# First product of three feed-forwards in seven half-size products for eight, in a fused two-block fp32 kernel on one core

## What is computed

```
def swiglu(h, w_in, w_out):
    a, b = h @ w_in[:, :D_FF], h @ w_in[:, D_FF:]      # D_FF = 2816, h is 512 x 1024
    return (silu(a) * b) @ w_out
```

## Time and profile before

| what | value |
|---|---|
| median of three executions | 3304.2 us (3299.51 to 3306.26) |
| span of the profiled execution | 3302.2 us |
| TensorE busy | 3203.2 us, 97% |
| VectorE, ScalarE, GpSimd busy | 48%, 34%, 13% |
| "ffn 0" on the trace | about 425 to 787 us |
| "ffn 1" | about 1136 to 1498 us |
| ("ffn2", 1) | about 2901 to 3281 us |

### The profile page before, as it was taken

The page is one execution under the profiler, slowest core; times in us unless marked ns, Lnnn a source line. Parts: engine busy times, 40 slices in busy tenths (PEclk is TensorE's granted clock), DMA queues, the critical chain, the costliest instruction groups (busy, mean ns, idle before and its releaser), DMA issues.

```text
span 3302.2 us, 45048 instructions
## 1 busy us (share of the span) xinstructions
PE 3203.2 (97%) x19414; PEld 2595.4 (79%) x19414; DVE 1573.5 (48%) x2498; ACT 1129.4 (34%) x1827; POOL 417.1 (13%) x622
## 2 busy tenths in 40 slices
PE   7999999999999999999999999999999999989999
PEld 5787888887887888887875677888887876668886
DVE  4646454446434654444246545343344437454544
ACT  6565532124434522223245443111112336431222
POOL 1302110002200300000010015000001311030000
PEclk9999999999999999999999999999999999999999
DMA  3111123223227322232243340222202222013221
GB/s 135 53 52 53 52 83 121 77 77 118 77 102 281 103 90 77 96 108 62 77 156 129 103 128 1 77 77 77 77 2 79 50 84 57 35 43 132 98 77 39
DMA packets 190743, 281.81 MB, mean 85 GB/s; under 512 B 19144, under 2 KB 122184, under 8 KB 190416
## 3 DMA queue, kind: packets, MB, share of 16 engines
q1 hardware_dynamic: 188368, 272.19, 24.8%
q10 hardware_dynamic: 2176, 6.73, 0.6%
HBM read 273.66 MB, written 2.10 MB: 84 GB/s over the span
## 4 chain that ended last, share of the span: by engine, by line
PE 90%; DVE 3%; ACT 3%; POOL 2%; issue 1%; DMA 1%; ACTq 0%; POOLq 0%; DVEq 0%; SPq 0%
PE ps L895 11%; PE ps L896 11%; PE ps L897 11%; PE ps L548 6%; PE ps L549 6%; PE ps L550 6%; PE ps L926 5%; PE ps L927 5%; PE ps L928 5%; PE ps L442 3%; PE ps L633 2%; PE ps L634 2%; PE ps L635 2%; PE ps L1533 2%; PE ps L1501 1%; PE ps L1709 1%
## 5 line engine op out<-in xcount | busy, mean ns | idle before, releaser
L451 ACT ACTIVATE R<-ring 128x2048 fp32r<-128x2048 f32 (+4 forms) x285 | 401.9, 1417 | 971.3 <-PE ps L928 345.0
L895 PE MATMUL ps<-R,R 128*128 128x512 f32 (+1 forms) x1760 | 654.3, 372 | 13.6 <-DVE R L810 8.6
L896 PE MATMUL ps<-R,R 128*128 128x512 f32 (+1 forms) x1760 | 650.3, 369 | 0.0
L897 PE MATMUL ps<-R,R 128*128 128x512 f32 (+1 forms) x1760 | 650.1, 369 | 0.0
L548 PE MATMUL ps<-R,R 128*128 128x512 f32 (+1 forms) x1016 | 395.9, 390 | 13.7 <-ACT U L451 4.0
L895 PEld LDWEIGHTS ps<-R,R 128*128 128x128 f32 x1760 | 333.2, 189 | 77.6 <-issue 13.0
L549 PE MATMUL ps<-R,R 128*128 128x512 f32 (+1 forms) x1016 | 379.2, 373 | 0.0
L550 PE MATMUL ps<-R,ringlo 128*128 128x512 f32 (+1 forms) x1016 | 378.4, 372 | 0.0
L897 PEld LDWEIGHTS ps<-R,R 128*128 128x128 f32 x1760 | 333.3, 189 | 56.2
L896 PEld LDWEIGHTS ps<-R,R 128*128 128x128 f32 x1760 | 333.4, 189 | 54.8 <-issue 0.5
L926 PE MATMUL ps<-R,R 128*128 128x512 f32 (+1 forms) x880 | 325.9, 370 | 0.9 <-DVE X L4029 0.9
(11 more groups left out here) (330 smaller groups left out, 4585.2 us busy)
## 6 DMA issues: line engine op xcount, KB each, us to landing
ring<-in_w_mod SPq DMA_DIRECT2D x24, 2048.0 KB, 9.8
ring<-in_ffn_w_in SPq DMA_DIRECT2D x44, 1024.0 KB, 11.9
ring<-in_w_ffn_in SPq DMA_DIRECT2D x44, 1024.0 KB, 12.2
ring<-in_ffn_w_out SPq DMA_DIRECT2D x10, 2048.0 KB, 8.0
ring<-in_w_ffn_out SPq DMA_DIRECT2D x10, 2048.0 KB, 8.0
ring<-in_dil_w_in SPq DMA_DIRECT2D x9, 2048.0 KB, 7.8
ring<-in_gdn_w_in SPq DMA_DIRECT2D x8, 2048.0 KB, 8.7
ring<-in_w_in SPq DMA_DIRECT2D x6, 1536.0 KB, 8.8
```

What stands on the lines that cost most here:

```text
L451: return act.e.activation(o, i, fn, **kw)
L895: pe.e.matmul(ps, w[0], x[0], start=(k == 0), stop=False)
L896: pe.e.matmul(ps, w[0], x[1], start=False, stop=False)
L897: t = pe.e.matmul(ps, w[1], x[0], start=False, stop=(k == 7))
```

## The change

"ffn 0", "ffn 1" and ("ffn2", 1) get functions of their own (`pe_ffn_s` and the like); ("ffn2", 0), with the context stream, stays. `FROM` says from which chunk on a chunk is made in the new way: chunk 2 in "ffn 0", chunk 3 in the other two. Chunks before it ("plain") are made as before, but with their own buffers `NT` for the high parts and the low part written in place into the ring slot.

From there on a chunk has two **units** (j = 0, 1). A unit takes the 2 x 2 blocks of the weights (k half by gate or other half) and of the activations (k half by 256-token half) and makes the four result blocks with seven products of 4 k-tiles by three matmuls of 128 x 256 instead of eight (Winograd's form): 84 half-width matmuls for 48 full-width ones. The seven weight factors are b11, b21, b22 of the weights themselves and t1 to t4, differences formed by GpSimd; the activation factors s1 to s4 are formed once for each feed-forward, in chunk FROM - 1, by VectorE and GpSimd. Products 1, 6, 7 and 4 pile up in one bank "a", and ScalarE copies ("snap") its state out between them; products 2, 5 and 3 have the banks "b", "c", "d", which VectorE adds in. Behind the seven products stand four output tiles of the chunk before.

```
+        def pe_unit(tag, c, j, between):
...
+            product(1, "a", True, False)
+            product(2, "b", True, True)
+            pe.wait_ge(*at("snap", tag, c, j, 0))
+            product(6, "a", False, False)
+            product(5, "c", True, True)
+            pe.wait_ge(*at("snap", tag, c, j, 1))
+            product(7, "a", False, False)
+            product(3, "d", True, True)
+            pe.wait_ge(*at("snap", tag, c, j, 2))
+            product(4, "a", False, True)
+            for i in range(4):
+                between(i)
+            if j:
+                pe.mark("gate up", tag, c)
+                pe.mark("ring read", (tag, "in", c))
```

GpSimd forms the factors of the next unit, ScalarE makes their high parts, VectorE the low parts:

```
+        def pool_factors(tag, c, j):
...
+            pool.wait_ge(*at("filled", (tag, "in", c)))
+            unit_free(pool, tag, c, j, 5)
+            op("t1", t1, b12, b11)
+            unit_free(pool, tag, c, j, 6)
+            pool.wait_ge(*at("factor", tag, c, j, "t1"))
+            op("t3", b12, b22, b12)
+            op("t2", t2, b22, t1)
+            pool.wait_ge(*at("factor", tag, c, j, "t2"))
+            op("t4", t4, b21, t2)
```

GpSimd's queue in the plain chunks and in the units (`unit_free` waits for "gate up" of the chunk when the unit before was plain):

```
+        def pool_ffn_s(tag, mid={}):
+            f = FROM[tag]
+            for c in range(f):
...
+                if c == f - 1:
+                    eng_shares(pool, tag, "s1")
+                    eng_shares(pool, tag, "s2")
+                pool_ffn_gate(tag, [S], c, 0, 0)
+                if (c, 1) in mid:
+                    mid[c, 1]()
+                if c == f - 1:
+                    eng_shares(pool, tag, "s4")
+                    pool_factors(tag, f, 0)
+                pool_ffn_gate(tag, [S], c, 1, 0)
+            for c in range(f, 11):
+                for j in range(2):
+                    pool_unit(tag, c, j, mid)
```

```
+        def dve_ffn_s(tag, take_out, then=None, early=None, mid={}, last=None):
...
+                if c == 0:
+                    dve_plain(tag, 1, 0)
+                if c == f - 1:
+                    eng_shares(dve, tag, "s3")
+                if c < f:
+                    dve_ffn_gate(tag, [S], c, 0, 0)
+                if 0 < c < f - 1:
+                    dve_plain(tag, c + 1, 0)
+                if c == f - 1:
+                    dve_share(tag, "s3")
+                    dve_share(tag, "s1")
+                if c < f:
+                    dve_ffn_gate(tag, [S], c, 1, 0)
+                elif c < 11:
+                    for j in range(2):
+                        dve_unit(tag, c, j, take_out)
+                if c < f - 1:
+                    dve_plain(tag, c + 1, 1)
+                if c in (0, 10):
+                    dve_out_lo(tag, c)
+                if c == 11 and early:
+                    early()
+                if c == 11:
+                    outs(10, border)
+                elif 0 < c < f:
+                    outs(c - 1)
+                if c == f - 1:
+                    dve_share(tag, "s2")
+                    dve_share(tag, "s4")
+                    for x in OPS:
+                        dve_factor(tag, f, 0, x)
+                if 0 < c < f:
+                    dve_out_lo(tag, c)
```

```
+        def act_out_hi(tag, c):
+            act.wait_ge(*at("filled", (tag, "out", c if c > 1 else 0)))
+            if c == 10:
+                act.wait_ge(*at("gate up", tag, 10))
+            elif c:
+                act.wait_ge(*at("down", tag, c - 1))
+            activate(WOH[c == 10], out_half(ring, tag, c), ACT.Copy).then_inc(*act.done("wo hi", tag, c))
```

More of the change, by code:

```diff
@@ L910, in pe_ffn_in @@
             pe.mark("gate up", tag, c)
+        FROM = {"ffn 0": 2, "ffn 1": 3, ("ffn2", 1): 3}
+        HALF = [slice(0, 256), slice(256, 512)]
+        NT = [[view(ru(o + 1024 * p, 1024), (8, 128)) for p in range(2)] for o in (22528, 28672)]
+        OPS = ("b11", "b21", "t2", "t1", "t3", "b22", "t4")
+        T_HI = {x: view(ru(o, 512), (4, 128)) for x, o in zip(
+            OPS, (22528, 23040, 23552, 24064, 28672, 29184, 29696))}
+        T_AT = {"t1": (31744, 31744), "t2": (32256, 32256), "t4": (8192, 30208)}
@@ new lines, in pe_unit, with product @@
+        def pe_unit(tag, c, j, between):
+            banks = {}
+            def product(i, x, first, last):
+                w, h = PRODUCTS[i]
+                if x not in banks:
+                    banks[x] = bank("sum", tag, c, j, x)
+                    PS.keep("sum", tag, c, j, x)
+                pe.wait_ge(*at("factor lo", tag, c, j, w))
+                if h in S_R:
+                    pe.wait_ge(*at("share lo", tag, h))
+                ps = banks[x][:, 0:256]
+                hi, lo = T_HI[w], factor(w, tag, c, j, True)
+                go_on = not first
+                for k in range(4):
+                    pe.e.matmul(ps, hi[:, k, :], share(h, 0)[:, k, :], start=(first and k == 0), stop=False, skip_group_check=go_on)
+                    pe.e.matmul(ps, hi[:, k, :], share(h, 1)[:, k, :], start=False, stop=False, skip_group_check=go_on)
+                    t = pe.e.matmul(ps, lo[:, k, :], share(h, 0)[:, k, :], start=False, stop=(k == 3), skip_group_check=go_on)
+                t.then_inc(*pe.done("unit", tag, c, j, i))
+                if last:
+                    PS.release("sum", tag, c, j, x)
+            product(1, "a", True, False)
[11 more added lines that the diff above has]
+            if j:
+                pe.mark("gate up", tag, c)
+                pe.mark("ring read", (tag, "in", c))
@@ new lines, in pe_out_one @@
+        def pe_out_one(tag, c, m, last):
+            ps = bank("product", tag, "out", c, m, 0)
+            pe.wait_ge(*at("wo lo", tag, c))
+            pe.wait_ge(*at("g lo", tag, c, 0, 1))
+            hi, lo = WOH[c == 10], out_half(ring_lo, tag, c)
+            for k in range(2):
+                w = [z[:, k, m * 128:(m + 1) * 128] for z in (hi, lo)]
+                x = [z[:, k, :] for z in GR_[0][c % 2]]
+                pe.e.matmul(ps, w[0], x[0], start=(k == 0), stop=False)
+                pe.e.matmul(ps, w[0], x[1], start=False, stop=False)
+                t = pe.e.matmul(ps, w[1], x[0], start=False, stop=(k == 1))
+            t.then_inc(*pe.done("product", tag, "out", c, m, 0))
+            if last and c == 10:
+                last(m)
+            if m == 7:
+                pe.mark("down", tag, c)
+                if c == 10:
+                    pe.mark("ring read", (tag, "out", 10))
+                    pe.mark("end", tag, "pe")
@@ new lines, in pe_ffn_s @@
+        def pe_ffn_s(tag, mid={}, between={}, last=None):
+            behind = (PS.i + 4) % 8
+            for c in range(12):
+                if c in mid:
+                    mid[c]()
+                if c == 0:
+                    pe_ffn_in(tag, [S], 0, between, 0)
+                elif c < FROM[tag]:
+                    pe_in_plain(tag, c)
+                elif c < 11:
+                    for j in range(2):
+                        pe_unit(tag, c, j, lambda i: pe_out_one(tag, c - 1, 4 * j + i, last))
+                    continue
+                if c:
+                    for m in range(8):
+                        pe_out_one(tag, c - 1, m, last)
+            while PS.i % 8 != behind:
+                PS.i += 1
@@ new lines, in act_plain, with dve_plain @@
+        def act_plain(tag, c, j):
+            for p in range(2):
+                act.wait_ge(*at("filled", (tag, "in", c)))
+                if c > 1:
+                    act.wait_ge(*at("product", "ffn", tag, c - 1, j, 0, 1))
+                elif j:
+                    act.wait_ge(*at("gate up", tag, 0))
+                activate(NT[j][p], column(ring, tag, c, j, p), ACT.Copy).then_inc(*act.done("plain hi", tag, c, j, p))
+        def dve_plain(tag, c, j):
+            for p in range(2):
+                dve.wait_ge(*at("plain hi", tag, c, j, p))
+                dve.e.tensor_tensor(column(ring_lo, tag, c, j, p), column(ring, tag, c, j, p), NT[j][p], SUB).then_inc(
+                    *dve.done("plain lo", tag, c, j, p))
@@ new lines, in pool_factors, with op @@
+        def pool_factors(tag, c, j):
+            def op(x, o, a_, b_):
+                pool.e.tensor_tensor(o, a_, b_, SUB).then_inc(*pool.done("factor", tag, c, j, x))
+            b11, b12, b21, b22 = (quarter(ring, tag, c, j, kh, p) for kh in range(2) for p in range(2))
+            t1, t2, t4 = (factor(x, tag, c, j, False) for x in ("t1", "t2", "t4"))
+            pool.wait_ge(*at("filled", (tag, "in", c)))
[7 more added lines that the diff above has]
+            op("t4", t4, b21, t2)
@@ L949, in dve_ffn_gate @@
             n, name = ns[s], (tag, c, j, s)
-            g, before = TG.take(*name)
+            if tag in FROM:
+                g, before = TG.tiles[j], TG.take_at([j], *name)[0]
+            else:
+                g, before = TG.take(*name)
             if c == 0 and tag in XRAW:
```

306 lines of the change are left out of this document (287 added, 19 removed).

## The result

| kernel | median | beside it, the kernel before | ratio, 95% interval |
|---|---|---|---|
| changed | 3325.7 us (3322.3 to 3328.4) | 3302.6 us | 1.0068 [1.0054, 1.0082] |

The account below looks back on a forecast made before the run. TensorE, busy 97% of the span, was taken to bound the kernel. Terms -41.0 - 0.7 + 13.7 + 14 + 18 + 10.5 + 9 = +23.5 on 3302.2, with 2 us to the median 3328; range 3294 to 3344.

Parts of the forecast that it names:

- 0.82 us a unit: In each unit's first product, 84 half-width matmuls replace 48 full-width: 10.88 to 10.06 us; 50 units, -41.0 us.
- units that stall: Rival: turns or snap 0 stall TensorE in each unit, from 0.15 us (3335) to 1 us (3378) and more; chance 0.12.
- half width at half price: Rival: 84 half-width matmuls in a row run at 0.1133 us, a unit saves 1.36, total 3301; chance 0.04.
- Last seams: Chunk 10 of each feed-forward: TensorE idles 4.55 us for the last second-product weights, three times; +13.7 us.
- first units of "ffn 1" and ("ffn2", 1): Before each first unit TensorE stands 4.0 us in "ffn 1" and 4.5 in ("ffn2", 1); +8.5 us.
- guests: Chunks 5, 7, 9 and 10 of "ffn 1": waits of 2.4, 1.3, 3.4 and 3.4 us behind guest work; +10.5, low 5.
- rival of cheap seams: GpSimd and VectorE meet less than laid out at the seams and chunk 1; total 3300; chance 0.25.
- chunk 1: Old 0.50 us stall in "ffn 0" goes, -0.7; the 5.09 us one of ("ffn2", 1) moves, 0, between -8 and +3.
- the clock: Granted clock falls behind six new stalls of 4 us and more, about 1.5 us each: +9, from 3 to 18.
- the bank waits of chunk 2: In "ffn 1" and ("ffn2", 1), VectorE's output tile 0 comes some 2.8 us after its bank is wanted; +5.6 or nothing.
- "ffn 0"'s first unit: At chunk 2 of "ffn 0", GpSimd and VectorE taking turns delay the start: +18 us, low 7, high 20.
- The chain over GpSimd's cast: First units of "ffn 1" and ("ffn2", 1): four factors, GpSimd's cast, then VectorE's low parts and output tiles, ending at G + 14.8.

Follow-up runs that it names:

- the half-width kernel: The kernel before with only the width changed: 25 chunks' first products made of 256-column matmuls instead of 512; 29.9 us more than the kernel before.
- the shares on VectorE: Changed kernel with weights' shares s1, s2 and s4 formed on VectorE instead of GpSimd; +13.3 us against the kernel before (changed kernel +23.1).
- GpSimd's order: Changed kernel with GpSimd's cast of the gated tile ahead of its four factors; +20.2 us against the kernel before (changed kernel +23.1).
- VectorE's order: Changed kernel with low parts s2, s4, b11 ahead of VectorE's eight output tiles, b21 and t2 between tiles 5 and 6; +10.2 us against the kernel before.
- the last seam: Changed kernel with chunk 10's second-product weights sent to a buffer free after the fifth product of unit (10,1); -1.3 us against the kernel before.
- the filled stalls: Changed kernel with unread 128-column matmuls on TensorE where it waits, at three first units and three last seams; +8.3 us against the kernel before.
- moving four things in three queues and one buffer: Changed kernel with new last weights' buffer, VectorE's order, shares on VectorE and guests moved within their chunks; 3275.9 us, 27.6 less than the kernel before.

## Why the prediction was right

**The gain.** 0.82 us a unit, and units that hold 15.5 us: both as forecast, the first shown by the half-width kernel too. The rivals of units that stall and of half width at half price are out.

**The seams.** Last seams, first units of "ffn 1" and ("ffn2", 1), and guests came within 0.3 us a term, because each was laid out as a queue with durations from rows. The rival of cheap seams is out as well: the first units with their bank waits, chunk 1 and the clock cost 42 us where it wanted them under 17.5.

**What was mis-sized.** The stalls sum to 47 us for 55.6: the bank waits of chunk 2 measured 2.0 and not 5.6 (with the shares on VectorE they are gone, as the forecast's cause for them has it), "ffn 0"'s first unit 14.8 and not 18, and the old stall of 2.3 at the end of "ffn 1" was not seen to go. The clock was 17 us and not 9. "Six at about 1.5" measured 1.8 when the six were filled; by the busy time at the lower level they and the 3.4 us stall ahead of "ffn 0"'s first unit took 14.8. The six shorter ones were counted at nothing, and of them the guests' stalls of 3.4 us in chunks 9 and 10 took 2.4 each (units of 12.3 us for 10.07, and what came before them). Against this, 2.7 us of the lower clock in the kernel before are gone. The two errors, 9 us too much for the stalls and 8 too little for the clock, nearly cancel. That 3328 lies within 2.3 us of the median is luck; without either error the sum would be 8 or 9 us off and still in the range.

**A step with the right size and half the cause.** The chain over GpSimd's cast gave 14.8 us for the first unit. GpSimd's order made next to no difference to it in "ffn 1" and ("ffn2", 1); a second chain, over TensorE's last output tile, ends at the same time, and only VectorE's order stands in both.

**What stays open.** In three experiments (the last seam, VectorE's order, the filled stalls) the medians fell by 4 to 7 us more than the spans of the traces, of which there is one for each kernel; what a single move gives is known no better than that. That a changed rotation of the banks made the new waits behind "ffn 0" is not shown.

## What to carry to other kernels

A saving on the bounding engine is kept only if each helper's queue is laid out again behind it: here 41 us saved became 23 lost, and moving four things in three queues and one buffer turned that into 28 gained. Look first where the shortened work used to cover a chain: the ends and the first steps of a loop, and the guests in it. Count each stall of TensorE of 3.4 us and more with some 2 us on top (1.6 to 2.8 here), and ask of each wait whether it is for work or for a buffer or place in a queue; most here were the second.

## What the runs showed of the hardware

In the changed kernel the clock's cost per stall did not grow with its length: the unit behind took 2.3 us more after 9.4 us of idle time at the first unit of "ffn 0" (12.40 us for 10.07), 2.5 after 3.7 in "ffn 1", 2.2 after 3.4 in chunk 9, and 1.6 after 4.2 in ("ffn2", 1) (11.62). Behind the stalls of 1.4 and 2.1 us in chunks 7 and 5 of "ffn 1" the clock did not fall. Idle TensorE time filled with unread matmuls of 128 columns, 0.23 us a call of two records, kept the clock at its upper level, so a kernel with 109 such calls more was the shorter one. One stretch of the trace was already at the lower level when its 20 fillers began (490 to 496 us, clock 0.55), and it was at the upper one before the first unit started at 497.07; in the changed kernel it rose only some 5 us after that unit's start.
